# Sample's index scores and 18 list rounds moved into the projection block, attention block reordered

## The reference, cut to what matters

```python
def indexer_scores(q_idx, w_idx, k_idx):
    s = relu(einsum('bthd,bsd->bths', q_idx, k_idx))
    return einsum('bths,bth->bts', s, w_idx)

def dsa_sample(q, k_new, v_new, q_idx, w_idx, kidx_new, cache_k, cache_v, cache_kidx, page_table, rel_bias):
    kidx_all = concatenate([cache_kidx[page_table], kidx_new])      # 2048 + 4 keys for each of 8 sequences
    sc = indexer_scores(q_idx, w_idx, kidx_all)                     # causal
    _, sel = top_k(sc, 256)
    # k, v of the selected keys (paged cache or new rows), bias by distance, softmax, sum
```

## Time and profile before

| | |
|---|---|
| median of 3 runs | 2160.57 us (2160.51 to 2166.61) |
| the profiled execution | 2160.03 us, its span 2158.3 us |
| TensorE busy | 1983.3 us (92%) |
| VectorE busy | 1591.0 us (74%) |
| ScalarE busy | 846.3 us (39%) |
| GpSimd busy | 581.5 us (27%) |
| projection block | to 374 us |
| attention block | 374 to 596 us |

### The profile page before, as it was taken

One profiled execution on the slowest core, in us unless ns is written; L12 is line 12 of the kernel. 1 busy time (PEld: TensorE's weight loads), 2 busy tenths in 40 slices (PEclk: granted clock), 3 DMA queues, 4 the chain that ended last, 5 costly groups with the idle time before them and its releaser, 6 DMA issues.

```text
span 2158.3 us, 32256 instructions
## 1 busy us (share of the span) xinstructions
PE 1983.3 (92%) x10400; PEld 1611.5 (75%) x10400; DVE 1591.0 (74%) x3167; ACT 846.3 (39%) x1721; POOL 581.5 (27%) x601
## 2 busy tenths in 40 slices
PE   8998998678879889999999899998969999999996
PEld 6774666334445558889999899998967888888885
DVE  4564265865323436889999989998958998988998
ACT  1232021223202321134777577667823333333331
POOL 1000133332200000002311222225635554544440
PEclk9998899878989999999999999999989999999998
DMA  6333232997750421448888899899999999999993
GB/s 218 77 73 125 83 102 80 362 361 268 280 235 3 154 71 59 135 129 265 312 268 261 277 300 312 260 315 382 392 353 393 398 404 380 387 387 388 381 385 134
DMA packets 240017, 547.45 MB, mean 254 GB/s; under 512 B 22350, under 2 KB 122511, under 8 KB 238474
## 3 DMA queue, kind: packets, MB, share of 16 engines
q1 hardware_dynamic: 179066, 337.23, 45.2%
q0 software_dynamic: 60816, 208.55, 26.5%
HBM read 485.08 MB, written 60.02 MB: 253 GB/s over the span
## 4 chain that ended last, share of the span: by engine, by line
PE 41%; DVE 12%; DMA 4%; issue 3%; ACT 2%; SPq 1%; DVEq 0%; ACTq 0%; POOLq 0%
PE psum L2933 22%; PE psum L2686 11%; PE psum L2206 5%; DVE u_gather L2580 3%; DMA u_raw<-in_uT 3%; PE psum L2702 2%; DVE uL L2332 1%; DVE hT L2612 1%; DMA S<-activation_table 1%; PE psum L2197 1%; SPq L2458 1%; DVE eq L2116 0%; DVE eq L2113 0%; ACT hT L2547 0%; DVE mv L1565 0%
## 5 line engine op out<-in xcount | busy, mean ns | idle before, releaser
L2322 POOL DMA_INDIRECT u_gather<-in_u_rows,gather_ids x160 | 194.3, 1214 | 804.1 <-DVE dots L2580 468.9
L2686 PE MATMUL psum<-hH,uH 128*128 128x384 f32 x1024 | 354.0, 346 | 6.2 <-DVE uL L2332 6.2
L2686 PE MATMUL psum<-hL,uH 128*128 128x384 f32 x1024 | 345.5, 337 | 0.0
L2686 PE MATMUL psum<-hH,uL 128*128 128x384 f32 x1024 | 345.2, 337 | 0.0
L2933 PE MATMUL psum<-vH,wH 128*128 128x512 f32 x768 | 301.3, 392 | 20.7 <-DVE wL L2877 20.7
L2933 PE MATMUL psum<-vH,wL 128*128 128x512 f32 x768 | 300.6, 391 | 0.0
L2933 PE MATMUL psum<-vL,wH 128*128 128x512 f32 x768 | 300.2, 391 | 0.0
L2795 POOL DMA_INDIRECT v_gather<-in_v_rows,idx_now x160 | 230.4, 1440 | 259.2 <-DVE y_sample L2884 160.1
L2580 DVE CUSTOM_DVE_ANT_0 u_gather<-u_gather,h 128x1024 f32<-128x1024 f32 x160 | 195.4, 1221 | 15.8 <-DMA u_gather<-in_u_rows,gather_ids 11.0
L2686 PEld LDWEIGHTS psum<-hH,uH 128*128 128x128 f32 x1024 | 194.6, 190 | 8.3 <-DVE uL L2332 8.1
L2686 PEld LDWEIGHTS psum<-hL,uH 128*128 128x128 f32 x1024 | 194.6, 190 | 0.0
(11 more groups left out here) (532 smaller groups left out, 3310.5 us busy)
## 6 DMA issues: line engine op xcount, KB each, us to landing
u_raw<-in_uT SPq DMA_DIRECT2D x128, 512.0 KB, 5.4
S<-in_v_rows SPq DMA_DIRECT2D x64, 512.0 KB, 12.2
v_rest<-in_v_rows SPq DMA_DIRECT2D x64, 512.0 KB, 6.7
activation_table<-acts SPq DMA_DIRECT2D x128, 192.0 KB, 4.9
gate_table<-Gtile SPq DMA_DIRECT2D x48, 512.0 KB, 6.6
S<-gate_table SPq DMA_DIRECT2D x16, 768.0 KB, 7.4
S<-activation_table SPq DMA_DIRECT2D x16, 768.0 KB, 13.0
G_rest<-gate_table SPq DMA_DIRECT2D x16, 768.0 KB, 8.3
```

The lines of the kernel that those rows point to most:

```text
L2322: c.nc.gpsimd.indirect_dma_start(c.ug[:, k % RG], None, c.A["u_rows"].rearrange("j i d -> (j i) d"), bass.IndirectOffsetOnAxis(ap=c.ids[:, ...
L2686: ins = nc.tensor.matmul(column[n % 4][:, 0:ND], w[:, n % RU, d], x[:, d], start=m == 0, stop=m == len(parts) - 1)
```

## The change

The sample's index scores leave the attention block and go into the projection block, in the middle of the k projections. VectorE runs 18 of the 32 list rounds there, and does none of tile 3's 16 rounds there any more (8 before). The index scores' working tiles lie in space that the SSD mixer is done with. POOL loads its 80 index pages in one go before it copies `qi_swapped`, and SP loads 12 pages after a block weight where it loaded 6. In the attention block the wait on `idx_mm` is gone, and k steps, v steps and masks stand at other places between the heads.

```diff
                     weights(i)
-                    load_kidx(c, sp, 6 * (i - 19), min(6 * (i - 18), KIDX_SP * NPAGE), c.ki_in)
+                    load_kidx(c, sp, 12 * (i - 19), min(12 * (i - 18), KIDX_SP * NPAGE), c.ki_in)
...
+                def sample_index():
+                    pe.wait_ge(ix["q_ready"], 1)
+                    pe.wait_ge(c.ki_in, 16 * KIDX_SP * NPAGE)
+                    pe.wait_ge(c.ki_in_pool, 16 * (NB - KIDX_SP) * NPAGE)
+                    pe.wait_ge(s["ho_ev"], 1)
...
+                    pe.wait_ge(ix["wx"], 1)
+                    pe.wait_ge(s["ynT_ev"], NTILE)
+                    for b in range(HB):
+                        ins = nc.tensor.matmul(bank[4][b * HT:(b + 1) * HT, 0:2], wx.rearrange("r h t -> r (h t)"),
+                                               c.bsel[:].rearrange("r (g b) -> r b g", g=2)[:, b],
+                                               start=True, stop=True)
+                    ins.then_inc(ix["wv_mm"], 1)
+                def sample_sums():
+                    pe.wait_ge(ix["w_ready"], 1)
+                    pe.wait_ge(ix["relu"], 2 * (NKC + 1))
+                    for g in range(2):
+                        for q in range(NKC):
+                            nc.tensor.matmul(bank[4][q * NS:(q + 1) * NS, :], Wsel[:, g],
+                                             part_scores[:, g, q * 512:(q + 1) * 512], start=g == 0, stop=g == 1)
+                    for g in range(2):
+                        ins = nc.tensor.matmul(bank[5][P - NS:P, 0:NS], Wsel[:, g], part_scores[:, g, PAST:NKEY],
+                                               start=g == 0, stop=g == 1)
+                    ins.then_inc(ix["sel_mm"], 1)
                 project("k", 1)
                 key_rows(0)
                 token_scores(2)
+                sample_index()
                 project("k", 2)
                 key_rows(1)
+                sample_sums()
                 project("k", 3)
                 key_rows(2)
...
                 relus(2)
+                sample_relus()
                 halves("k", 2, c.kT[:, 2])
                 key_rows(1)
+                sample_past()
                 halves("k", 3, c.kT[:, 3])
...
+                def sample_queries():
+                    qi = qiS.rearrange("d r par (k two) t -> d par two k r t", two=2)
+                    link(V.memset(qiS, 0.0))
+                    dve.wait_ge(c.swap_in, 32)
...
+                def sample_weights():
+                    dve.wait_ge(ix["wv_mm"], 1)
...
+                def sample_list():
+                    dve.wait_ge(ix["sel_mm"], 1)
...
                 pick_rounds(c, link, score[1], 1, 0, 16)
+                sample_queries()
                 accumulate(2)
-                pick_rounds(c, link, score[2], 2, 0, 16)
+                pick_rounds(c, link, score[2], 2, 0, 8)
+                sample_weights()
+                pick_rounds(c, link, score[2], 2, 8, 16)
                 accumulate(3)
-                pick_rounds(c, link, score[3], 3, 0, 8)
+                sample_list()
+                sample_rounds(c, link, 0, ROUNDS_IN_FRONT)
...
-                load_kidx(c, pool, NB // 2 * NPAGE, (NB - 1) * NPAGE, c.ki_in_pool)
+                load_kidx(c, pool, NB // 2 * NPAGE, NB * NPAGE, c.ki_in_pool)
                 pool.wait_ge(s["ns_ev"], NB)
+                pool.dma_start(sel_const, A["att_const"][:, 0:NSEL]).then_inc(ix["const"], 16)
+                load_kidx(c, pool, KIDX_SP * NPAGE, NB // 2 * NPAGE, c.ki_in_pool)
+                pool.wait_ge(f["emptied"], at[("qi", 3, 1)] + 1)
+                for lo in (0, HD):
+                    pool.dma_start(c.swapped[lo:lo + HD], c.qiT[HD - lo:P - lo, :, SEQ:NT]).then_inc(c.swap_in, 16)
...
-                    if j == 0:
-                        for lo in (0, HD):
-                            pool.dma_start(c.swapped[lo:lo + HD],
-                                           c.qiT[HD - lo:P - lo, :, SEQ:NT]).then_inc(c.swap_in, 16)
-                    if j == 1:
-                        load_kidx(c, pool, (NB - 1) * NPAGE, NB * NPAGE, c.ki_in_pool)
-                    if j == 2:
-                        load_kidx(c, pool, KIDX_SP * NPAGE, NB // 2 * NPAGE, c.ki_in_pool)
...
                 if n >= KV_RING:
                     eng.wait_ge(*used((n - KV_RING) // HB))
-                elif n >= 4:
-                    eng.wait_ge(z["idx_mm"], 2 * (NKC + 1))
...
-                sample_scores()
+                far_bias()
+                qk(0, 0)
+                qk(0, 1)
                 k_step(0)
                 k_step(1)
-                qk(0, 0)
-                qk(0, 1)
-                k_step(2)
-                k_step(3)
-                attend(0, {0: ((k_step, 4), (k_step, 5)), 1: ((k_step, 6), (k_step, 7)),
-                           2: ((k_step, 8), (k_step, 9), (k_step, 10))})
-                k_step(11)
-                k_step(12)
+                attend(0, {0: ((k_step, 2), (k_step, 3)), 1: ((k_step, 4), (k_step, 5)), 2: ((k_step, 6),)})
+                k_step(7)
                 sample_limits()
-                k_step(13)
+                k_step(8)
                 sample_masks(0)
-                k_step(14)
+                k_step(9)
                 turn_out(0)
-                attend(1, {0: ((k_step, 15), (sample_turn, 0), (v_step, 0)), 1: ((sample_masks, 1), (v_step, 1)),
-                           2: ((v_step, 2),), 3: ((v_step, 3),)})
+                attend(1, {0: ((k_step, 10),), 1: ((k_step, 11),), 2: ((k_step, 12),), 3: ((k_step, 13),)})
                 turn_out(1)
-                attend(2, {0: ((v_step, 4),), 1: ((v_step, 5),), 2: ((v_step, 6),), 3: ((v_step, 7),)})
+                attend(2, {0: ((k_step, 14),), 1: ((k_step, 15), (sample_turn, 0)),
+                           2: ((v_step, 0), (sample_masks, 1)), 3: ((v_step, 1),)})
                 turn_out(2)
-                sample_turn(1)
-                v_step(8)
-                attend(3, {0: ((v_step, 9),), 1: ((v_step, 10),), 2: ((v_step, 11),), 3: ((v_step, 12),)})
+                attend(3, {0: ((v_step, 2), (v_step, 3)), 1: ((v_step, 4), (v_step, 5)),
+                           2: ((v_step, 6), (v_step, 7)), 3: ((sample_turn, 1), (v_step, 8))})
                 turn_out(3)
+                for i in range(9, 12):
+                    v_step(i)
                 sample_out(0)
-                for i in range(13, 2 * NST):
+                for i in range(12, 2 * NST):
                     v_step(i)
                 sample_out(1)
...
-                sample_weights()
-                sample_list()
-                sample_rounds(0, 8)
+                def rounds(first, end):
+                    sample_rounds(c, link, first, end)
+                F = ROUNDS_IN_FRONT
+                rounds(F, F + 2)
+                sample_setup()
                 dve.wait_ge(s["T_in"], 16)
-                attend(0, {1: (sample_rounds, 8, 16), 3: (sample_rounds, 16, 24), 5: (sample_rounds, 24, stop_k // 8)})
+                attend(0, {1: (rounds, F + 2, F + 6), 3: (rounds, F + 6, F + 10), 5: (rounds, F + 10, stop_k // 8)})
                 sample_threshold()
                 scale_out(0)
                 sample_mask()
                 mask_logits(0)
-                attend(1, {5: (mask_logits, 1), 7: (last_rounds, 8, 10)})
+                attend(1, {1: (last_rounds, 0, 3), 3: (last_rounds, 3, 6), 5: (last_rounds, 6, 8), 7: (last_rounds, 8, 10)})
                 scale_out(1)
-                attend(2, {1: (last_rounds, 10, 12), 3: (last_rounds, 12, 14), 5: (last_rounds, 14, 16)})
+                attend(2, {1: (last_rounds, 10, 12), 3: (last_rounds, 12, 14), 5: (last_rounds, 14, 16),
+                           7: (mask_logits, 1)})
                 scale_out(2)
```

## The result

The changed kernel takes **2246.84 us** (median; 2242.11 to 2250.11) against 2160.54 of the kernel before: a ratio of 1.0387, interval 1.0363 to 1.0410. The forecast was 2214 with a range to 2226: the direction was right, the size not, and no rival reached it either (the highest, C, ended at 2227). The profiled execution has a span of 2247.8 us, 89.5 more than before.

| | block starts | attention | rest | span |
|---|---|---|---|---|
| before | 374.25 | 221.73 | 1562.32 | 2158.3 |
| after | 433.01 | 247.52 | 1567.27 | 2247.8 |
| difference | +58.8 | +25.8 | +5.0 | +89.5 |
| forecast | +61.8 | -8 | 0 | +53.8 |

A forecast was written before the change was run, and what follows sets the result against it. Transfers were taken to bound attention's first half, TensorE to run to the projection block's end, the page queue to bound nothing before. 2160.0 + 61.8 (later start) - 8 (attention) = 2213.8, median 2214; range 2203 to 2222, 8 of 10 2188 to 2226.

The forecast's parts named there:

- Step 1: Projection block: POOL's 80 pages at 1.15 us delay the qi_swapped copies to 351.2, so VectorE stands still 41.7 us.
- Step 2: Rest of the projection block after the stop: VectorE ends at 432.3, attention starts at 436, +61.8 us.
- rival D: Projection block: stop shorter, only copies or only pages matter; 424.5 against 432.3, 2206 us; chance 0.06 with mixtures to 2180.
- Step 3: Attention block, 221.7 us before: forecast at 214, a change of -8 us (-39 to +5).
- Removed: index scores and list rounds: Attention block: loses the index scores, 18 list rounds (28.5 us of VectorE) and the wait until 386.30.
- The lower bound: Attention block with transfers full throughout: step 0 near T + 12, then 5.49 us a step, 190.7 us in all.
- the walk: Attention block followed through its new order: k steps 0 and 1 about T + 14, threshold T + 45, end T + 216.
- Walk, from tile 3 on: End of attention: tile 3 at T + 140, v 4 at T + 147, 11 steps at 5.49, end T + 216.
- The 8 rounds of tile 3: Attention tiles 1 and 2: 8 more VectorE rounds, one k step less, 66 us where 70 before.
- A: Attention block: stop stays but transfers are full, attention 182 to 191, time 2191 (2183); chance 0.14.
- B: Projection block: POOL's queue not the limit, pages under 0.67 us each; 2148 or 2171 us; chance 0.08, 0.06 faster.
- C: Attention block: reordered steps wait more, masks hold the ring, tile 3 last and long; 222 to 227, time 2222 to 2227; chance 0.10.

The follow-up runs named there:

- e2: Changed kernel with index keys loaded as one 512 KB transfer per sequence, 8 loads for 128, page table left out; 2212.3 us, ratio 1.0247.
- e8: e7 with index scores behind tile 3's scores, 9 list rounds and tile 3's 8 rounds in the projection block, attention order as before; 2185.0 us, ratio 1.0110.
- e1: Changed kernel with POOL's constants and the two qi_swapped copies behind its first 24 index pages instead of all 80; 2233.7 us, ratio 1.0336.
- e3: Changed kernel with TensorE's and ScalarE's attention order put back, VectorE's mask of group 1 back in tile 1; 2224.9 us, ratio 1.0303.
- n1: Kernel before with only the new attention order of k and v steps, turns and masks; 2204.3 us, ratio 1.0197.
- e6: e3 with all attention orders as before, tile 3's 8 rounds and 10 list rounds instead of 18 in the projection block; 2222.7 us, ratio 1.0277.
- e7: e1 with index pages split 64 and 64 between SP and POOL instead of 48 and 80; 2229.4 us, ratio 1.0289.
- c3: Kernel before with 14 of tile 3's rounds in the projection block and v steps moved earlier, two left behind tile 3; 2161.5 us, ratio 0.9993.

## Why the prediction was wrong, step by step

**Step 1, right.** The second copy starts near 348.5 (347.84 and half of 1.27; 348.3 forecast), VectorE waits 41.22 us (41.7), from the queue's 1.15 us per load. e2 shows that the loads' number does it. The Trainium skill, "DMA: Bandwidth & Descriptors", section "Anatomy of one DMA", fits a POOL transfer to 2.0 us plus bytes / 436e3. Taken as 75 ns for each 32 KB page behind the other, which is an estimate from that fit, it would have put the copies near 260 us; the trace has them at 347.84 and sides against that use of it for this loop.

**Step 2, right.** Scores of tile 3 at 393.60 (393.4 forecast), ScalarE's end at 424.77 (424.6), VectorE's at 432.5 (432.3). The next block starts at 433.01 and not at 436, since the boundary took 0.5 us and not 3.7; it took 0.5 in e8 too (393.47 to 393.97), where VectorE is last as well. e1's 425.95 bears out rival D's pricing of the second wait (424.5 + the boundary). That the sums agree to 0.2 us is in part luck: they count from POOL's first page, which lay at 252.3 before and 252.6 after, but at 248.1 in e3. One reading is off and harmless: between the scores of tiles 2 and 3 TensorE makes two rows of k and not three, in the 23.8 us that were read from the trace.

**Step 3, wrong: forecast -8, measured +25.8.** Two terms of it failed, the start of the block and above all what stands behind tile 3; a third held.

*Removed: index scores and list rounds.* The lower bound put step 0 near T + 12 and went on from there, taking the old release at 386.30 for a loss. Step 0 did come at T + 11.0, but step 1 at T + 24.9, where the bound implied T + 17.5 and the walk had both steps by T + 14; the threshold at T + 51.5, not T + 45. Three steps, the bias tile and the constants share the transfers, which are full from 4 us on; after:

```profile
437.00:441.00 4.00, 1.31 (x6) 1.00 (x6) 2.71 (x11) 0.00 (x0) 1.71 (x4) 0.50 1.00 364
450.00:458.00 8.00, 0.10 (x4) 0.12 (x8) 5.80 (x16) 0.00 (x0) 1.45 (x3) 0.53 1.04 387
```

What the trace of before has, and the forecast left out, is the DMA share in 378 to 386 us: 0.96 and 1.05. By e8 the whole removal is worth nothing in the old order (221.8 against 221.7).

*Walk, from tile 3 on.* Tile 3 came at T + 147.7 (T + 140 forecast), 6.5 of it from the start. Then "v 4 can't land before its slot is released plus 10.0, so T + 147, and 11 more steps at 5.49" took transfers for the only limit inside tile 3. But v 4 stands behind tile 3's second pair of heads, and v 8 behind the whole tile and the turn of group 1: they ran at T + 169.2 and T + 202.4, and on the way there the ring was full twice (3 GB/s at 589 us, 67 GB/s at 631). So v 4 was 22 us later than forecast, v 15 came at T + 237.0 instead of T + 207.5, and 2 more lie between it and the next block: 31.5 us over the forecast of T + 216. The prediction's remark that one step per pair of heads gives most of the early start back named the mechanism but not its size; it gave back more than all of it, and turned the block's sign. e3 takes the order away, -16.6, and n1 brings it alone, +36.9. The new order costs less in the changed kernel than in n1: without the list rounds its tile 0, whose length is VectorE's in that order, is 21 us shorter (T + 79.8 against T + 100.4).

*The 8 rounds of tile 3, right.* They were inside "66" for tiles 1 and 2, and those took 67.9. In the old order e6 puts them, exchanged for list rounds, at 6.0 us.

These sum up, in single profiles: 221.7 + 16.6 (order) + 6.0 (rounds) + 3.2 (e6's remainder) = 247.5. The remainder isn't that three steps share the transfers at the start: e8 lets them do so too, with the same attention code, and takes 221.8. It is of the size of the scatter.

**The clock.** Part of the order's price varies between executions. e1, e2 and e7 have the changed kernel's attention code and took 244.6, 238.0 and 238.1 us. From tile 3's start to v 8 the changed kernel needs 54.7 us, e2 44.9. The windows of that stretch, after:

```profile
577.00:583.00 6.00, 4.81 (x24) 1.20 (x16) 1.32 (x4) 0.60 (x1) 1.07 (x2) 0.73 0.19 51
583.00:589.00 6.00, 4.27 (x15) 2.47 (x15) 3.20 (x9) 2.20 (x6) 1.07 (x3) 0.55 0.84 300
595.00:601.00 6.00, 6.00 (x39) 2.40 (x31) 0.91 (x2) 1.03 (x2) 2.14 (x4) 0.81 0.48 156
```

and e2, 31 us earlier in time:

```profile
546.00:552.00 6.00, 5.38 (x25) 1.37 (x24) 1.19 (x3) 0.60 (x1) 0.54 (x1) 0.69 0.09 17
552.00:558.00 6.00, 3.71 (x26) 2.75 (x27) 4.48 (x12) 2.87 (x7) 1.61 (x3) 1.00 0.89 311
558.00:564.00 6.00, 6.00 (x48) 2.37 (x48) 1.73 (x5) 2.06 (x5) 1.07 (x2) 1.00 0.39 115
```

In both, the granted clock was at 0.50, the lower level of 1.2 GHz, in the 6 us before the first of these windows, behind 18 us in which TensorE was busy for 15.3. In both it came back near tile 3's start. In e2 it stayed at full to 570 us; in the changed kernel it fell again some 3 us into tile 3 (0.55 in 583 to 589) and was low until about 597, and again from about 618 to 633, so that v 2 took 3.64 us where in e2 it takes 1.92. Up to 9.5 of the 25.8 us is this, and the forecast had no such term. It also bounds what e3 can tell: against the 238.0 of e2 the order would be worth 7.1 us in the changed kernel, not 16.6. n1 against the kernel before is the firmer pair, 36.9 us in the profiles and 40.7 in the medians. What decides between the two courses stays open.

**Rivals.** A (transfers full) is refuted by the windows (0.72, 0.01 and 0.18 above), B (queue not the limit) by 1.15 us a load, D by the start at 433. C, "masks hold the ring, tile 3 is last and long", named the right mechanism and capped it at 227: the cap was a round figure, not worked out from the steps that stand behind tile 3.

## What to carry to other kernels

When work leaves a block, look at what was full beside it in its own window: here the transfers were, and removing 12 us of TensorE work brought attention nothing (221.8 against 221.7), while the same work cost 10.4 us in a block that TensorE bounds (e8). Before moving loads ahead of something on a queue, multiply their number by the start-to-start spacing, not by one record's duration, and list every wait that stands behind it. In a pipeline with a ring, count how many steps stand behind the last long piece of other work: the block's end came 45.1 us after v 8 with seven behind it, and 20.6 us after v 12 with three, however early the rest ran. That has an end: going from three to two brought nothing (c3), since the steps placed earlier waited for their transfers instead.

## What was not expected of the hardware

With the pages split evenly between SP and POOL, the weights that share SP's queue came late: a wait of 7.78 us for a weight block in e8. Whole loads of 512 KB took 18.3 to 26.7 us to land against other traffic, and a weight block came 10.4 us late beside them, so e2 recovered 31 us of the stop and not all. And one attention code showed lengths from 238.0 to 247.5 us with TensorE's granted clock in its tile 3 (0.72 from T + 148 to T + 200 in the longest, 0.93 in the shortest).
